# Two-layer sequence model on one core: input products one tile later, half of the condition blocks in the gate stage, the first chunk's outputs between the last two projections

## The chip, the cores and the metric

One Trainium2 chip, one of its cores. The metric is the device time of one execution in microseconds (us), the median of several runs. Engines: PE (TensorE, matrix products), DVE (VectorE), ACT (ScalarE), POOL (GpSimd), and SP, which only issues transfers. "PEld" is PE's weight load, a trailing q (SPq, ACTq) is the queue of an engine that issues DMAs.

## The reference

One sequence of 512 tokens of width 1024 in float32 goes through a gated delta-rule mixer, a SwiGLU feed-forward, an S5 mixer, a mixture of eight experts, and then two attention layers. The change touches the feed-forward, the S5 mixer and the gate behind it, and it computes the conditions of the two attention layers elsewhere:

```python
u = x @ w_in                                        # "projections"
a_bar = exp(lam * dt); bu = b_bar @ u               # per group: 16 channels, 64 complex states
h = associative scan of h[t] = a_bar * h[t-1] + bu[t]
y = real(c @ h) + d_skip * u
hid = gelu(y); val, gate = split(hid @ w_glu, 2)    # gate stage
x = layer_norm(ALPHA * x + val * sigmoid(gate))     # then router and experts
mods[layer] = silu(c) @ w_ada[layer] + b_ada[layer] # "condition", for attention layers 0 and 1
```

## The kernel before, in words

The kernel is a chain of stages. A stage (`Stage`) has one program for each engine; engines meet at its end. Semaphores (`then_inc`, `wait_ge`) order the engines inside it, and each engine works through its program strictly in the order in which it is written.

Matrix products of float32 precision are made in three passes (`three_pass`, L260 to L267): every weight tile is split into a high half (ACT, `split_hi`) and a low half (DVE, `split_lo`), and PE multiplies high by high, high by low and low by high. A weight tile that has no low half yet holds PE up.

**Feed-forward stage** (`dense_parts`, L2711). Two parts of 18 tiles each: 12 tiles "up" and 6 "down", numbered as splits 0 to 35. Beside the splits DVE does the work of `Parameters` (L1739), which prepares the S5 stage: after the low half of split n (`vector`, L1849) it does `condition` (blocks of the condition product: a 128x1024 piece of `w_ada` times `silu(c)` with a sum, L1975, two per split from split 9 on, 48 in all for both layers), and at the splits named in `Q_AT` and `P_AT` one of eight Q tables (`output_powers`, L1926) or P tables (`input_powers`, L1947). SP (`loads`, L2912) waits for each low half, then for the blocks and tables of that split, and issues their loads and stores and the next weight tile in that order. At the end `EndNorm` (L2632) normalizes the four token tiles one by one (`spread`, `centre` on DVE, `root` and `high_parts` on ACT, `turn` on PE, `low_parts` on DVE), and the last `turn` needs the last tile's norm.

**S5 stage** (`s5_layer`, L2025). Eight projections (`project`, L2092: one weight tile each, 24 matmuls), whose results ACT copies out (`copy_u`) and sends through DRAM to get them turned (`u_turn`, then `u_blk`, read back by SP's `turn_u`). Four chunks b follow, each with: `turn_tables` (16 transposes of its P table, inside a projection when `project` is given b), `inputs` (64 matmuls), `lags` (32), `outputs` (96) and `turn_back` (8 transposes). DVE scans the states (`turn_in`, `scan`, `turn_out`) and before that makes the rotation tables (`skip_diagonals`, `rotations`). POOL (`widen`, `zero`, `add_skip`) and SP (`place`) lay the lags out in `mix` by eight small DMAs each per chunk, which `outputs` reads. ACT fetches each chunk's P table (`next_tables`, once `inputs` of the chunk before are done) and Q block (`load_q`). PE's order is written out in L2157 to L2184.

**Gate stage** (`router`, L3405). Eight weight tiles (`s5_glu`), each multiplied with four token tiles; DVE does the low halves and the gated sums (`add`), then for the last chunk the norm (`spread`, `centre`), the router's logits and the slot lists. ACT does the sigmoids (`gate`). POOL has nothing to do in it.

`keep_busy` (L191) issues matmuls whose result nobody reads; each call is two records of a 128x384 product.

## Time and profile before

| | |
|---|---|
| median of 3 runs | 2575.66 us (2573.46 to 2578.72) |
| profiled execution, its own time | 2578.13 us |
| its span | 2576.4 us |
| PE busy | 2467.8 us, 96% of the span |
| DVE busy | 1740.6 us, 68% |
| ACT busy | 1044.0 us, 41% |
| POOL busy | 603.0 us, 23% |
| feed-forward stage | until about 844 us |
| S5 stage | 844 to 970 us |
| gate stage | 970 to 1082 us |

PE is busy nearly throughout, so the kernel's time is PE's work plus the holes in it, plus what PE takes longer where its granted clock is at the lower level. The views to read are therefore PE's waits by stage, and the timeline of the other engines just before each hole. Times in a timeline are counted from the start of the span; in brackets stands how long the engine was idle before and who released it.

### The profile page before, as it was taken

What the parts mean: (1) busy time and instruction counts of PE and PEld (TensorE: products, weight loads), DVE (VectorE), ACT (ScalarE), POOL (GpSimd) and SP (SyncE); (2) the same over time, 40 slices, a digit from 0 to 9 for tenths busy, and PEclk for the clock granted to TensorE, in tenths of its full rate; (3) what the DMA queues carried; (4) which work ended last, traced back from release to release, by engine and by line L of the source; (5) the groups of instructions that cost most, each with busy time, mean ns of one, the idle gap of its engine ahead of it and who ended that gap; (6) DMA issues with size and microseconds to landing.
All of it is one profiled execution on the core that took longest, in us unless ns stands there. A gap on an engine that the chain in (4) does not pass through costs nothing. (4 is left out here: it accounts for less than half of the span.)

```text
span 2576.4 us, 40971 instructions
## 1 busy us (share of the span) xinstructions
PE 2467.8 (96%) x15793; PEld 2031.6 (79%) x15793; DVE 1740.6 (68%) x2854; ACT 1044.0 (41%) x1561; POOL 603.0 (23%) x481
## 2 busy tenths in 40 slices
PE   8998989999999899899999999998999998999998
PEld 7788887787878689799999999886676576767576
DVE  7944656468888743666766766676687567487666
ACT  4443233331211342455555555443344452344453
POOL 2404321430230140142333432430024001024001
PEclk9999999999999899999999999999999999999999
DMA  4321002347664552367777777843221211332121
GB/s 156 91 89 36 2 3 66 118 137 259 207 212 162 183 157 85 105 224 238 239 250 228 235 244 228 287 167 125 86 74 60 76 68 56 110 94 70 33 82 66
DMA packets 265197, 348.33 MB, mean 135 GB/s; under 512 B 23184, under 2 KB 221008, under 8 KB 264528
## 3 DMA queue, kind: packets, MB, share of 16 engines
q1 hardware_dynamic: 253872, 313.81, 37.6%
q0 software_dynamic: 5536, 17.17, 2.0%
q10 hardware_dynamic: 5632, 15.21, 1.8%
q8 instruction: 104, 1.70, 0.3%
q14 instruction: 53, 0.43, 0.0%
HBM read 322.83 MB, written 20.71 MB: 133 GB/s over the span
## 5 line engine op out<-in xcount | busy, mean ns | idle before, releaser
L3057 PE MATMUL ps<-x_feat_r,moe_w_hi 128*128 128x384 f32 x1408 | 405.2, 361 | 2.6 <-DVE x_feat_r L3169 2.6
L2587 DVE TENSOR_TENSOR moe_w_lo<-ring,moe_w_hi 128x2048 fp32r<-128x2048 f32 x144 | 316.8, 2201 | 130.3 <-ACT moe_w_hi L2582 130.1
L3060 PE MATMUL ps<-x_feat_r,moe_w_lo 128*128 128x192 f32 x1408 | 354.0, 251 | 0.0
L2582 ACT ACTIVATE moe_w_hi<-ring 128x2048 fp32r<-128x2048 f32 x144 | 254.8, 1770 | 97.5 <-PE ps L263 60.8
L3060 PEld LDWEIGHTS ps<-x_feat_r,moe_w_lo 128*128 128x128 f32 x1408 | 269.2, 191 | 0.3
L3057 PEld LDWEIGHTS ps<-x_feat_r,moe_w_hi 128*128 128x128 f32 x1408 | 264.3, 188 | 3.7 <-issue 3.4
L267 PE MATMUL ps<-x_free_r,ring_r 128*128 128x512 f32 x496 | 195.6, 394 | 0.0
L266 PE MATMUL ps<-ring_r,x_feat_r 128*128 128x256 f32 (+2 forms) x576 | 183.9, 319 | 0.0
L263 PE MATMUL ps<-x_feat_r,ffn_w_hi 128*128 128x512 f32 x352 | 139.7, 397 | 1.2 <-DVE ffn_w_lo L2530 1.2
L267 PE MATMUL ps<-x_feat_r,ffn_w_lo 128*128 128x512 f32 x352 | 139.5, 396 | 0.0
L266 PE MATMUL ps<-x_free_r,ffn_w_hi 128*128 128x512 f32 x352 | 138.3, 393 | 0.0
L2582 ACT ACTIVATE ffn_w_hi<-ring 128x2048 fp32r<-128x2048 f32 (+1 forms) x35 | 61.8, 1769 | 176.3 <-PE ps L263 149.6
L4098 ACT ACTIVATE s_sb<-s_sb,att_small 128x512 f32<-128x512 f32 (+3 forms) x128 | 71.9, 562 | 133.2 <-DVE att_small L4090 133.0
L266 PEld LDWEIGHTS ps<-ring_r,x_feat_r 128*128 128x128 f32 x576 | 108.7, 189 | 7.8
L267 PEld LDWEIGHTS ps<-x_free_r,ring_r 128*128 128x128 f32 x496 | 93.1, 188 | 21.1
L3105 ACT ACTIVATE moe_cross<-ps 128x384 f32<-128x384 f32 (+1 forms) x96 | 44.4, 462 | 150.8 <-PE ps L3060 150.8
L263 PE MATMUL ps<-x_feat_r,acc_r 128*128 128x512 f32 x256 | 103.4, 404 | 0.0
L267 PE MATMUL ps<-x_feat_r,ring_r 128*128 128x512 f32 x256 | 101.7, 397 | 0.0
L266 PE MATMUL ps<-x_free_r,acc_r 128*128 128x512 f32 x256 | 101.6, 397 | 0.0
L3288 POOL TENSOR_TENSOR moe_hid_hi<-moe_prod,cst 128x384 fp32r<-128x384 f32 (+1 forms) x48 | 54.5, 1134 | 195.3 <-DVE moe_prod L3232 195.3
L4366 POOL TENSOR_TENSOR sq<-c_all 128x512 f32<-128x512 f32 x16 | 19.7, 1232 | 342.9 <-ACT c_all L3974 342.9
L194 PE MATMUL ps<-cst 128*128 128x384 f32 x226 | 83.7, 518 | 15.8 <-PEq L175 13.7
(654 smaller groups left out, 6401.9 us busy)
## 6 DMA issues: line engine op xcount, KB each, us to landing
ring<-in_moe_w SPq DMA_DIRECT2D x120, 1024.0 KB, 8.6
ring<-in_w_in SPq DMA_DIRECT2D x32, 1024.0 KB, 5.3
ring<-in_ffn_w SPq DMA_DIRECT2D x30, 1024.0 KB, 7.8
ring<-in_ada_t SPq DMA_DIRECT2D x48, 512.0 KB, 4.6
ring<-in_gdn_w_in SPq DMA_DIRECT2D x12, 1024.0 KB, 5.7
ring<-in_moe_w SPq DMA_DIRECT2D x24, 512.0 KB
ring<-in_s_w_glu SPq DMA_DIRECT2D x8, 1024.0 KB, 5.9
ring<-in_w_out SPq DMA_DIRECT2D x8, 1024.0 KB, 6.7
```

The lines of the kernel that those rows point to most:

```text
L194: prog.nc.tensor.matmul(prog.ps[:, bank, 0:3 * P], prog.ident, prog.cst, start=True, stop=True)
L263: m = nc.tensor.matmul(out, lh, rh, start=first, stop=False)
L266: nc.tensor.matmul(out, lh, rl, start=False, stop=False)
L267: return nc.tensor.matmul(out, ll, rh, start=False, stop=last)
L2582: self.prog.nc.scalar.activation(self.flat(self.hi, j % SPLITS, j), self.raw(j), ACT.Copy).then_inc(self.hi_done, 1)
L2587: self.prog.nc.vector.tensor_tensor(self.flat(self.lo, j % SPLITS, j), self.raw(j), self.flat(self.hi, j % SPLITS, j).bitcast(F32), ALU.su ...
L3057: mm = nc.tensor.matmul(out, wh[:, k, cs], both[:, k, :], start=(k == 0), stop=False)
L3060: mm = nc.tensor.matmul(out[:, 0:SLOTS], wl[:, k, cs], xg[0][:, k, :], start=False, stop=(k == KD - 1))
L3105: nc.scalar.activation(cross_of(c, which), half(c, which, 1), ACT.Copy).then_inc(cross_copied, 1)
L3288: nc.gpsimd.tensor_tensor(hi, src, prog.ones[:, 0:1].unsqueeze(2).to_broadcast([P, len(ms), SLOTS]), ALU.mult).then_inc(hi_ready, 1)
L4098: self.nc.scalar.activation(x, x, ACT.Exp, bias=self.small[:, u % 4, 1:2], scale=self.heads[h][3], accum_out=self.small[:, u % 4, 2:3]).th ...
L4366: m = nc.gpsimd.tensor_tensor(sq[:, 0 if first else 1, :], c_all[:, k, :], c_all[:, k, :], ALU.mult)
```

## The change

It does six things.

- `Parameters` computes only layer 0's 24 condition blocks, one per split (9 to 32), and the Q and P tables move to other splits; the first P table goes from split 11 to 13.
- `input_powers` walks its arrays with the channel innermost instead of the step.
- In `EndNorm`, ACT and DVE also split the S5 stage's first weight tile, and PE issues eleven `keep_busy` calls ahead of the last `turn`; the two at the head of the S5 stage go.
- In the S5 stage PE's order is: projections 0, 1, 2 (with chunk 0's tables), 3, `inputs(0)`, `lags(0)`, 4, 5 (tables 1), `inputs(1)`, `lags(1)`, 6, `outputs(0)`, 7 (tables 2), `inputs(2)`, `lags(2)`, tables 3 on their own, `turn_back(0)`, `inputs(3)` and the rest as before. ACT, DVE and SP follow.
- The gate stage gets layer 1's 24 condition blocks: POOL loads them, one DMA each into two buffers, DVE multiplies them in six groups of four, one group behind each low half from tile 2 to tile 7, and `finish_conditions` stands ahead of the norm.
- ACT applies silu to the condition row once more in the gate stage.

```diff
@@ Parameters
-    FIRST_SPLIT, PER_SPLIT = 9, 2
-    Q_AT = {9: 0, 13: 1, 17: 2, 20: 3, 23: 4, 26: 5, 29: 6, 32: 7}
-    P_AT = {11: 0, 15: 1, 19: 2, 22: 3, 25: 4, 28: 5, 31: 6, 34: 7}
+    FIRST_SPLIT = 9
+    Q_AT = {9: 0, 14: 1, 17: 2, 20: 3, 22: 4, 24: 5, 26: 6, 31: 7}
+    P_AT = {13: 0, 16: 1, 19: 2, 21: 3, 23: 4, 25: 5, 27: 6, 33: 7}
     def blocks_at(self, split):
-        first = (split - self.FIRST_SPLIT) * self.PER_SPLIT
-        return range(max(first, 0), min(max(first + self.PER_SPLIT, 0), DEPTH * self.BLOCKS))
+        n = split - self.FIRST_SPLIT
+        return range(n, n + 1) if 0 <= n < COND_BLOCKS else ()
@@ input_powers
-        shape = [P, self.QUADS, GC, STEP]
+        shape = [P, self.QUADS, STEP, GC]
...
-        p_re, p_im, tmp = self.p[:, 0], self.p[:, 1], self.p_tmp
+        p_re, p_im, tmp = (x.rearrange("p q c i -> p q i c") for x in (self.p[:, 0], self.p[:, 1], self.p_tmp))
@@ new, used by both stages (COND_BLOCKS is 24)
+def condition_block(prog, layer, n, weights, row):
+    return prog.nc.vector.scalar_tensor_tensor(out=weights, in0=weights, scalar=1.0, in1=row, op0=ALU.mult, op1=ALU.mult,
+                                               accum_out=prog.mods[:, layer, n:n + 1])
+def finish_conditions(prog, link, layer):
+    nc, mods, scale = prog.nc, prog.mods[:, layer, :], prog.mods[:, layer, KD:2 * KD]
+    link(nc.vector.tensor_tensor(mods, mods, prog.ada_par[:, layer, :], ALU.add))
+    link(nc.vector.tensor_scalar(scale, scale, 1.0, None, ALU.add))
@@ s5_layer, PE
-            keep_busy(prog, 7, 2)
             project(0)
             project(1)
             project(2, 0)
+            project(3)
             inputs(0)
-            project(3)
-            project(4, 1, lambda half: table_bank_free(0, half))
+            lags(0, lambda half: table_bank_free(0, half))
+            project(4)
+            project(5, 1, lag_bank_free)
             inputs(1)
-            lags(0, lambda half: table_bank_free(1, half))
-            project(5)
-            project(6, 2, lag_bank_free)
+            lags(1, lambda half: table_bank_free(1, half))
+            project(6)
+            outputs(0)
+            project(7, 2, lambda half: lag_bank_free(2 + half))
             inputs(2)
-            lags(1, lambda half: table_bank_free(2, half))
-            project(7, 3, lambda half: lag_bank_free(2 + half))
-            lags(2, lambda half: table_bank_free(3, half))
-            outputs(0)
-            turn_back(0, lambda half: lag_bank_free(4 + half))
+            lags(2, lambda half: table_bank_free(2, half))
+            turn_tables(3, 0, lambda half: lag_bank_free(4 + half))
+            turn_tables(3, 1, lambda half: pe.wait_ge(t_copied, 12 + half + 1))
+            turn_back(0, lambda half: table_bank_free(3, half))
             inputs(3)
@@ s5_layer, ACT (rewritten between copy_tables(0) and finish(0); only the new order)
+            copy_tables(0); copy_u(2); proj.split_hi(act, 5); copy_u(3); proj.split_hi(act, 6)
+            next_tables(1); load_q(1); copy_lags(0); copy_u(4); proj.split_hi(act, 7); copy_tables(1); copy_u(5)
+            next_tables(2); load_q(2); copy_lags(1); copy_u(6); copy_y(0); load_q(3); copy_tables(2); copy_u(7)
+            next_tables(3); copy_lags(2); copy_tables(3); finish(0)
@@ s5_layer, DVE
-            for n in range(3):
-                proj.split_lo(dve, n)
+            dve.sem_inc(proj.lo_done, 1)
+            proj.split_lo(dve, 1)
+            proj.split_lo(dve, 2)
             skip_diagonals()
             rotations()
             proj.split_lo(dve, 3)
             proj.split_lo(dve, 4)
+            proj.split_lo(dve, 5)
             turn_in(0)
-            proj.split_lo(dve, 5)
+            proj.split_lo(dve, 6)
             scan(0)
             turn_out(0)
-            proj.split_lo(dve, 6)
+            proj.split_lo(dve, 7)
@@ s5_layer, SP
             turn_u(5)
+            place(1)
             turn_u(6)
-            place(1)
             turn_u(7)
@@ EndNorm (ACT, DVE) and the end of the feed-forward stage (PE)
+    def split_next_hi(self, act):
...
+        self.nc.scalar.activation(self.next_hi, W.flat(NEXT, 0)[0], ACT.Copy).then_inc(self.next_hi_done, 1)
+    def split_next_lo(self, dve):
...
+        self.nc.vector.tensor_tensor(lo, x, self.next_hi.bitcast(F32), ALU.subtract)
...
+                pe.wait_ge(by_token.low_done, 2)
+                keep_busy(prog, 0, 11)
                 by_token.turn(pe, NT - 1)
@@ router, DVE
+                def conditions(first, count):
+                    for n in range(first, first + count):
+                        if n == 0:
+                            dve.wait_ge(silu_row, 1)
+                        dve.wait_ge(cond_landed[n % 2], 16 * (n // 2 + 1))
+                        condition_block(prog, DEPTH - 1, n, cond_w[:, n % 2, :], cond_row).then_inc(cond_used, 1)
+                each = COND_BLOCKS // (2 * LAST)
                 for c in range(LAST):
                     tiles.split_lo(dve, 2 * c + 2)
+                    conditions(2 * c * each, each)
...
                     tiles.split_lo(dve, 2 * c + 3)
+                    conditions((2 * c + 1) * each, each)
+                dve.wait_ge(cond_used, COND_BLOCKS)
+                finish_conditions(prog, link, DEPTH - 1)
@@ router, POOL
+                pool.dma_start(cond_row, inp["ada_c"]).then_inc(row_landed, 16)
+                for n in range(COND_BLOCKS):
+                    if n >= 2:
+                        pool.wait_ge(cond_used, n - 1)
+                    pool.dma_start(cond_w[:, n % 2, :], inp["ada_t"][DEPTH - 1, n * P:(n + 1) * P, :]
+                                   ).then_inc(cond_landed[n % 2], 16)
```

## Rows read from the trace of the kernel before

**Rows 1.** What TensorE (PE) waited for, 500 to 836 us: total us, times, longest

```profile
PE ps L263 <- DVE ffn_w_lo L2587: 4.4, 2, 2.9
```

**Rows 2.** Timeline of PE: start us, us, engine line op, out<-in, xcount, idle before

```profile
585.45 0.50 PE L263 MATMUL ps<-ffn_w_hi,ffn_hid_hi 128*128 128x512 f32 x1 [2.88 <-DVE ffn_w_lo L2587]
...
836.21 1.03 PE L2663 MATMUL ps<-cst,x_tok 128*128 128x128 f32 x8
...
846.75 1.11 PE L263 MATMUL ps<-x_feat_r,acc_r 128*128 128x512 f32 x1
...
963.66 6.62 PE L194 MATMUL ps<-cst 128*128 128x384 f32 x20
```

**Rows 3.** Windows of 2 us: PE, PEld, DVE, ACT, POOL busy (x), granted clock, DMA

```profile
586.00:588.00 2.00, 2.00 (x8) 1.57 (x7) 2.00 (x3) 1.91 (x1) 1.93 (x1) 0.72 0.00 0
588.00:590.00 2.00, 2.00 (x7) 1.51 (x6) 2.00 (x3) 0.00 (x0) 1.92 (x2) 0.50 0.82 231
590.00:592.00 2.00, 2.00 (x10) 1.64 (x9) 2.00 (x1) 0.00 (x0) 0.24 (x1) 0.93 0.63 147
```

**Rows 4.** What PE waited for, 836 to 975 us, columns as in Rows 1

```profile
PE ps L2109 <- DMA s_ublk<-u_turn: 6.5, 2, 3.4
PE ps L2663 <- DVE x_tok L2689: 3.7, 1, 3.7
...
PE ps L2154 <- ACT acc L2226: 1.4, 2, 0.7
PE ps L2122 <- POOLq L2404: 0.7, 1, 0.7
```

**Rows 5.** Timeline of ACT and PE in the S5 stage

```profile
854.07 1.11 ACT L2209 ACTIVATE s_uring<-ps 128x512 f32<-128x512 f32 x1 [5.03 <-PE ps L267]
...
859.62 1.13 ACT L2209 ACTIVATE s_uring<-ps 128x512 f32<-128x512 f32 x1 [2.88 <-PE ps L267]
...
870.29 3.56 PE L2109 MATMUL ps<-s_ublk,s_into 128*64 128x64 f32 x64 [3.45 <-DMA s_ublk<-u_turn]
...
910.07 2.09 PE L2109 MATMUL ps<-s_ublk,s_into 128*64 128x64 f32 x64
```

**Rows 6.** Timeline of DVE in the S5 stage

```profile
850.40 0.22 DVE L2314 TENSOR_TENSOR s_pow<-cst 128x64 f32<-128x64 f32 x1
...
868.40 2.36 DVE L3895 TENSOR_TENSOR ring_r<-ring,acc_r 128x1024 fp32r<-128x1024 f32 x2
```

**Rows 7.** Timeline of DVE in the feed-forward stage

```profile
573.16 2.06 DVE L1975 SCALAR_TENSOR_TENSOR ring<-ring,x_tok 128x1024 f32<-128x1024 f32 x1
...
577.40 1.13 DVE L1959 TENSOR_TENSOR x_tok<-s_bbar,s_pow 128x512 f32<-128x512 f32 x1
...
579.61 0.69 DVE L1961 TENSOR_TENSOR x_tok<-x_tok 128x512 f32<-128x512 f32 x1
...
814.42 0.69 DVE L2881 TENSOR_TENSOR acc<-ps,acc 128x512 f32<-128x512 f32 x1 [5.13 <-DMA s_p<-x_tok]
```

**Rows 8.** Timeline of DVE: a block in the feed-forward stage, then the gate stage

```profile
603.63 1.22 DVE L1975 SCALAR_TENSOR_TENSOR ring<-ring,x_tok 128x1024 f32<-128x1024 f32 x1
...
985.91 2.29 DVE L242 TENSOR_TENSOR ring_r<-ring,s_glu_hi 128x2048 fp32r<-128x2048 f32 x1 [9.04 <-ACT s_glu_hi L234]
989.85 0.42 DVE L3566 TENSOR_TENSOR s_sig<-s_sig,ps 128x256 f32<-128x256 f32 x1 [1.65 <-ACT s_sig L3680]
...
1043.16 2.29 DVE L242 TENSOR_TENSOR ring_r<-ring,s_glu_hi 128x2048 fp32r<-128x2048 f32 x1 [0.41 <-ACT s_glu_hi L234]
1049.70 0.42 DVE L3566 TENSOR_TENSOR s_sig<-s_sig,ps 128x256 f32<-128x256 f32 x1 [4.25 <-ACT s_sig L3680]
```

**Rows 9.** DMA issues of the whole execution: count, KB each, median us to landing

```profile
ring<-in_ada_t SPq DMA_DIRECT2D x48, 512.0 KB, 4.6
...
s_into<-s_p ACTq DMA_DIRECT2D x4, 1024.0 KB, 5.4
y_rows<-moe_y POOLq DMA_DIRECT2D x7, 512.0 KB, 3.5
```

More of the change, by code:

```diff
@@ L1951, in input_powers @@
         quad = slice(n * self.QUADS, (n + 1) * self.QUADS)
[L1952 to L1955 removed]
+        shape = [P, self.QUADS, STEP, GC]
+        b_re, b_im = (self.s5.bbar[:, r, quad, :].unsqueeze(2).to_broadcast(shape) for r in range(2))
+        re, im = (self.s5.pw[:, r, 1:].rearrange("p i q -> p q i")[:, quad, :].unsqueeze(3).to_broadcast(shape) for r in range(2))
+        p_re, p_im, tmp = (x.rearrange("p q c i -> p q i c") for x in (self.p[:, 0], self.p[:, 1], self.p_tmp))
         dve.wait_ge(self.q_done, n + 1)
@@ L1974, in condition @@
             dve.wait_ge(self.weights_landed[n % 2], 16 * (n // 2 + 1))
-            nc.vector.scalar_tensor_tensor(out=self.weights[n % 2], in0=self.weights[n % 2], scalar=1.0, in1=self.row,
-                                           op0=ALU.mult, op1=ALU.mult, accum_out=mods[:, layer, i:i + 1]
-                                           ).then_inc(self.weights_used, 1)
-            if n == DEPTH * self.BLOCKS - 1:
+            condition_block(self.prog, 0, n, self.weights[n % 2], self.row).then_inc(self.weights_used, 1)
+            if n == COND_BLOCKS - 1:
                 dve.wait_ge(self.weights_used, n + 1)
                 dve.wait_ge(self.bias_landed, 16)
-                link(nc.vector.tensor_tensor(mods, mods, self.prog.ada_par, ALU.add))
-                for l in range(DEPTH):
-                    scale = mods[:, l, KD:2 * KD]
-                    m = nc.vector.tensor_scalar(scale, scale, 1.0, None, ALU.add)
-                link(m)
+                finish_conditions(self.prog, self.linked(dve), 0)
+COND_BLOCKS = 3 * D // P
+def condition_block(prog, layer, n, weights, row):
[5 more added lines that the diff above has]
+    link(nc.vector.tensor_scalar(scale, scale, 1.0, None, ALU.add))
 def load_turned(sp, u_dram, u_blk, f, landed):
@@ L2629, in parts_of @@
             yield e
+NEXT = "s5_u"
 class EndNorm:
@@ L2644, in __init__ @@
         names = ("gamma_landed", "beta_landed", "norm_link", "var_ready", "sd_ready", "centred", "normed", "turned", "x_hi_done",
-                 "measured")
+                 "measured", "low_done", "next_hi_done")
         (self.gamma_landed, self.beta_landed, self.norm_link, self.var_ready, self.sd_ready, self.centred, self.normed,
-         self.turned, self.x_hi_done, self.measured) = (st.counter(n) for n in names)
+         self.turned, self.x_hi_done, self.measured, self.low_done, self.next_hi_done) = (st.counter(n) for n in names)
         self.link = None
+        self.next_hi = prog.split_scratch[:, 0, 0:D]
+    def split_next_hi(self, act):
+        W = self.prog.weights
+        act.wait_ge(self.normed, 1)
+        W.arrived(act, NEXT, 0)
+        self.nc.scalar.activation(self.next_hi, W.flat(NEXT, 0)[0], ACT.Copy).then_inc(self.next_hi_done, 1)
+    def split_next_lo(self, dve):
+        x, lo = self.prog.weights.flat(NEXT, 0)
+        dve.wait_ge(self.next_hi_done, 1)
+        self.nc.vector.tensor_tensor(lo, x, self.next_hi.bitcast(F32), ALU.subtract)
     def loads(self, sp):
@@ L2828, in scalar @@
                         end.high_parts(act, t - 1)
+                    if t == NT - 2:
+                        end.split_next_hi(act)
                 end.high_parts(act, NT - 1)
@@ L2886, in vector @@
                         end.low_parts(dve, t - 1)
+                    if t == NT - 2:
+                        end.split_next_lo(dve)
                 end.low_parts(dve, NT - 1)
@@ L3425, in router @@
         sig = prog.sbuf("s5_sig", [P, 2, UP_COLS], own)
+        cond_row = prog.sbuf("cond_row", [P, D], own)[:, :]
+        cond_w = prog.sbuf("cond_w", [P, 2, D], own)
         turned_logits = prog.sbuf("moe_turned", [EXPERTS, NT, P], own)
@@ L3459, in router @@
             pick, token, spot = gather
+            row_landed, silu_row, cond_used = st.counter("row_landed"), st.counter("silu_row"), st.counter("cond_used")
+            cond_landed = [st.counter(f"cond_landed_{i}") for i in range(2)]
             late = slice(0, SLOTS - P)
@@ L3695, in _ @@
                 tiles.split_hi(act, 1)
+                act.wait_ge(row_landed, 16)
+                nc.scalar.activation(cond_row, cond_row, ACT.Silu).then_inc(silu_row, 1)
                 for c in range(LAST):
```

43 lines of the change are left out of this document (17 added, 26 removed).

## The prediction

> **What bounds the kernel now.** I read three views, in this order: what TensorE (PE) waited for in each stage, then the timeline around each wait, then the windows with the granted clock. From 500 to 836 us, in the dense feed-forward stage, PE waits for one thing only: twice, 4.4 us together, for the low half of a weight tile that VectorE (DVE) makes late [rows 1]. The first of these stalls, 2.88 us, ends at 585.45, so the second is 1.5 us [rows 2]. Behind the first the granted clock is at the lower of its two levels, 1.2 GHz, for about 3.3 us (0.72, 0.50 and 0.93 in windows of 2 us) [rows 3]: some 1.7 us more. In the S5 stage the waits are 6.5 us in two for the turned input `u_blk`, 3.7 us for the norm of the last token tile, and small ones [rows 4]. So in both stages PE sets the end, and DVE or a transfer makes the holes. In the gate stage (`s5_glu`, 970 to 1082 us) PE is full until about 1067 us, DVE half idle at first, but from 1049.70 on DVE runs the norm, the router and the slot lists in one chain [rows 8]. A delay of DVE there is a delay of the kernel.
>
> **Feed-forward stage: fewer condition blocks, P tables elsewhere.** Before, the split that stalls PE was queued behind two blocks (2.06 and about 2.3 us) and a whole P table [rows 7]. Now one block stands there, and the first P table comes two splits later: the low half, which ended at 585.4, ends near 577.5, before PE's 582.6. The second stall is the same pattern (two blocks and Q number 6 ahead of it); the new lists leave splits 28 to 30 with one block each. What is late next at both places is the last product of the chunk, which the next matmuls need only 2.8 us (12 matmuls) on: no new wait. The Q and P tables now sit closer, in pairs from split 19 to 27. Per two tiles (22.2 us of PE) DVE has two splits, two blocks, a P and a Q and two products, some 20 us: it fits. The P table's new loop order writes with a stride where it read with one. No row has this pattern; a step lies between the 0.69 us of the contiguous one and the 1.13 us of the strided read [rows 7], so a table costs 4.2 to 6.8 us against 5.8. I take 5.8, and it is covered by DVE's slack of 2 us per pair at any value but the last. SP's stores follow the tables; the last one, for which DVE stood 5.13 us [rows 7], goes out some 15 us earlier, which PE does not feel. Sum: -2.9 - 1.5 - 1.7 = **-6.1 us** (bounds -6.6 and -4.4, the latter if the slow clock stays).
>
> **Into S5: eleven filler matmuls before the last turn.** Twenty records of the filler, ten calls, last 6.62 us [rows 2], so eleven last 7.3. They start behind turn(2), at 837.0, and end at 844.3, while the last tile's norm (delayed 0.4 us by the added 1.2 us split of the next tile, since DVE had 0.9 us of slack) is ready at 841.2. The last turn thus ends at 845.3 instead of 842.9, and the stage opens 2.7 us later, at 847.2. In exchange the first projection, which began at 846.75 on the lower clock [rows 2], finds its tile split already and runs at 2.4 GHz: 847.2 + 5.55 = 852.8 against 854.07 [rows 5], **-1.3 us** there.
>
> **S5: where the wait goes.** One projection is 5.55 us (854.07 to 859.62) and one with a chunk's tables inside 7.2 (859.62 to 866.84) [rows 5]. Projections 0, 1 and 2 end at 865.6. The new order puts projection 3 next, not the inputs, so the wait for `u_blk` is covered. But projection 3 needs the low half of tile 3, which DVE's program makes behind `skip_diagonals` and `rotations`: these took 18.0 us, from 850.4 to 868.4 [rows 6]. DVE now gets there at 851.8 (2.4 us later by the turn, 1.1 earlier because tile 0's pieces are gone), is through at 869.8, and tile 3 is ready at 871.0. PE waits **5.4 us**, in place of 3.45, and comes out on the lower clock: the 64 input matmuls behind the old hole took 3.56 us against 2.09 [rows 5], so 1.5 us again. Downstream: lags(1) needs GpSimd's (POOL's) second `widen`, which stands behind eight DMA issues: about 0.4 us. The tables of the fourth chunk no longer hide in projection 7. Their load is issued once inputs(2) are done, at 923.6, and takes 5.4 us [rows 9]; PE is through lags(2) at 927.2, so 1.9 us of waiting, and 0.8 us more because nothing fills the copies between their transposes. Sum of the new holes: 5.4 + 1.5 + 0.4 + 1.9 + 0.8 = 10.0. The old holes, all gone: 6.5 + twice 1.5 of clock + 0.7 (lags(2) on POOL) + 0.7 (the copy of y, which the outputs moved forward cover) = 10.9 [rows 4, 5]. With the -1.3 the stage gives **-2.2 us** (bounds -5, if the hole costs no clock and the load of tables lands in the 3.5 us that others take, and +1, if it stays slow for twice as long). On the queues: ACT now reads the tables of chunk 1 behind inputs(0), still 6 us ahead of their transposes, and the last Q blocks 18 us sooner; SP places chunk 1 ahead of `turn_u(6)`, which only inputs(3) need. Further on the lags of chunk 3 set the end by the same twelve us as before, and outputs(0) waits for nothing, because POOL and SP placed its lags 7 us earlier.
>
> **Gate stage: 24 blocks, loaded through POOL.** One block is 1.15 us of DVE, start to start, where POOL computes nothing [rows 8]; a group of four would be 4.6. But there are two buffers, and the load of block n+2 is issued only when block n has been read. The trace shows no load through POOL's queue; a store of the same 512 KB through it lands after 3.5 us, a block through SP's after 4.6 as median [rows 9]. I take 3.5, since it is the row of that queue and this stretch is quieter than that of the 4.6. The third block's load goes at 1.3 and lands at 4.8, the block ends at 5.95; the fourth, issued at 2.45, lands at 6.0 and ends at 7.2. So a group is **7.2 us**. From 988.2, where tile 2's low half ends, DVE has in a row: 6 groups 43.2, five splits of 2.29 = 11.5, twelve pairs of 0.42 + 0.43 = 10.1, the statistics 2.4, small ones 0.5, `finish_conditions` 0.6, together 68.3: it comes to the last chunk's sum at 1056.5, and with 0.4 to 0.7 us of further landing waits at 1057.2 instead of 1049.70 [rows 8]. On the way PE's last tile (its low half was ready at 1045.45) comes 3 us late, which costs nothing of its own, as DVE is later still. **+7.5 us.** Lower bound: loads land in time. Then DVE is bound by PE as before up to 1045.45, and only the last group and the finish, less the 4.25 us that DVE idled there, are added: +1.0. Upper: 4.6 us to landing, by the same walk +16. The Trainium skill, DMA: Bandwidth & Descriptors, section on the anatomy of a DMA on the gpsimd path, fits such a DMA as 2.0 us plus its bytes at 436 GB/s; for 512 KB that is 3.2 us (an estimate by that page), where the row says 3.5. By it the groups would cost 5.6 us in place of 7.5.
>
> **Sum.** -6.1 - 2.2 + 7.5 = -0.8 us. The profiled execution took 2578.13 us (span 2576.4), 2.5 above the median of 2575.66; it becomes 2577.3, and the median **2575 us**. What a measurement here tells from no change is about 0.2%, 5.2 us.
>
> **Rivals.** (1) The loads through POOL are never waited for: they land within 2.3 us, or as good as. Then -6.1 - 2.2 + 1.0 = -7.3: 2568.4. Against it, no 512 KB row lands so soon; for it, the stretch is quiet. 0.15. (2) No hole at projection 3, because DVE's rotations or the opening of the stage come sooner than I worked out, with the gate stage as in the forecast: 5.4 + 1.5 gone, -7.7: 2568.0. Against it the 18.0 us of [rows 6], a fixed run of DVE work. 0.15. (3) **Slower**: the second load of each pair shares the 16 engines with the first and with the gate weights and lands after 4.2 us or more. Groups become 7.9 to 8.3 us, tile 5 is late as well as tile 7, and the stage costs +13 to +16: total +5 to +8, 2581 to 2584. It decides from a landing of 4.2 us on; the 4.6 us median of SP's blocks speaks for it, the 3.5 of POOL's queue against. 0.24. (4) The change doesn't reach the path at all (the holes of DVE's lateness stay, the added work is hidden), a result near zero, goes with the forecast.
>
> **Chances.** Forecast and what lies within 5.2 us of no change 0.46; faster 0.30; slower 0.24. The range reaches to rival 1 with a little of the S5 bound, 2566.5, and into rival 3, 2583.
>
> **What would show it.** The two PE waits for `ffn_w_lo` gone; PE full until 844 us (less 6) with the clock at its higher level at the first projection; a PE wait of some 5 us for `ring_r` (L3895) before the fourth projection in place of those for `s_ublk`; a wait of 2 us for `s_into`; in the gate stage DVE waits for DMA, twice in each group, summing to some 15 us, and the router's chain 7 us later against its stage's start. It is wrong if DVE's rows show no wait for `cond_w`, or if PE enters the fourth projection without a hole.

## The result and the profile after

| | before | after |
|---|---|---|
| median, runs taken side by side | 2576.91 us | 2594.52 us |
| range of these runs | 2573.46 to 2578.72 | 2590.21 to 2597.23 |
| profiled execution, its span | 2576.4 us | 2590.8 us |
| first product of S5 | 846.75 | 841.38 |
| first product of the gate stage | 971.96 | 966.53 |
| last chunk's first gated sum | 1049.70 | 1064.40 |
| first product of the experts | 1096.34 | 1109.55 |

The changed kernel takes 1.0071 times as long, 95% interval 1.0058 to 1.0083: 17.6 us by the medians, 14.4 us between the two profiled executions. The forecast was 2575 us, no change. The four marks at the foot of the table, read from the two timelines, and the two spans say where it went: 5.4 us are gained by the time S5 starts and are kept through S5; the gate stage then loses 20.1 us (97.87 us from its first product to the last chunk's sum, against 77.74), of which 1.5 come back before the experts start; 1.2 are added in the rest.

In the feed-forward stage the two waits of [rows 1] are gone: the list of PE's waits from 500 to 830 us is empty. PE's waits from 836 to 975 us, after (total us, times, longest), against [rows 4]:

```profile
PE ps L263 <- DVE ring_r L3945: 5.5, 1, 5.5
PE ps L2092 <- DMA s_into<-s_p: 2.2, 1, 2.2
PE ps L263 <- DVEq L2372: 1.9, 1, 1.9
...
PE ps L2157 <- ACT acc L2230: 0.7, 1, 0.7
```

The waits for `s_ublk` are gone, and two new ones stand there, for the low half of tile 3 and for the fourth chunk's tables. The timeline of PE at the opening and at the first of these holes, with the windows around it (columns as in Rows 2 and 3), against [rows 2, 5]:

```profile
831.35 7.26 PE L194 MATMUL ps<-cst 128*128 128x384 f32 x22
838.45 1.04 PE L2684 MATMUL ps<-cst,x_tok 128*128 128x128 f32 x8
841.38 0.50 PE L263 MATMUL ps<-x_feat_r,acc_r 128*128 128x512 f32 x1 [1.90 <-DVEq L2372]
...
865.40 0.77 PE L263 MATMUL ps<-x_feat_r,acc_r 128*128 128x512 f32 x1 [5.47 <-DVE ring_r L3945]
...
873.67 2.09 PE L2112 MATMUL ps<-s_ublk,s_into 128*64 128x64 f32 x64
```

```profile
864.00:866.00 2.00, 0.60 (x2) 0.54 (x3) 1.97 (x2) 0.00 (x0) 0.00 (x0) 0.52 0.28 98
866.00:868.00 2.00, 2.00 (x6) 1.62 (x5) 1.92 (x4) 0.00 (x0) 0.00 (x0) 0.50 0.43 99
868.00:870.00 2.00, 2.00 (x6) 1.52 (x6) 0.00 (x0) 0.00 (x0) 0.00 (x0) 0.50 0.19 40
870.00:872.00 2.00, 2.00 (x9) 1.60 (x8) 0.00 (x0) 0.00 (x0) 0.00 (x0) 0.77 0.00 0
```

S5 now opens at the higher clock: its first matmul takes 0.50 us, where it was 1.11 in [rows 2]. Behind the hole the clock is at the lower level until about 871, so the fourth projection takes 873.67 - 865.40 = 8.27 us instead of 5.55.

The gate stage, DVE's waits from 975 to 1064 us, and the second group of four blocks on the timeline, with POOL's issues between DVE's rows, against [rows 8, 9]:

```profile
DVE cond_w L1981 <- DMA cond_w<-in_ada_t: 27.9, 15, 4.2
```

```profile
997.59 1.22 DVE L1981 SCALAR_TENSOR_TENSOR cond_w<-cond_w,cond_row 128x1024 f32<-128x1024 f32 x1
...
999.11 0.53 POOL L3717 DMA_DIRECT2D cond_w<-in_ada_t  x1 [6.80 <-DVE cond_w L1981]
...
1000.26 0.53 POOL L3717 DMA_DIRECT2D cond_w<-in_ada_t  x1 [0.62 <-DVE cond_w L1981]
1003.52 1.23 DVE L1981 SCALAR_TENSOR_TENSOR cond_w<-cond_w,cond_row 128x1024 f32<-128x1024 f32 x1 [3.56 <-DMA cond_w<-in_ada_t]
...
1005.56 1.23 DVE L1981 SCALAR_TENSOR_TENSOR cond_w<-cond_w,cond_row 128x1024 f32<-128x1024 f32 x1 [0.81 <-DMA cond_w<-in_ada_t]
```

The first two blocks are there. (That isn't so in the third and fifth group, which start right behind the one before.) The load of the third is issued at 999.11, 1.5 us into the group, and lands 4.4 us later; that of the fourth, at 1000.26, 5.3 later. The group ends at 1006.71, 9.1 us after its start. The six groups take 8.7, 9.1, 12.7, 8.6, 9.0 and 8.5 us. PE feels it twice, and behind both waits the granted clock is 0.50 (from 1028 to 1034 us and from 1054 to 1058):

```profile
1029.52 0.58 PE L263 MATMUL ps<-s_glu_hi,x_feat_r 128*128 128x256 f32 x1 [5.66 <-DVE ring_r L242]
...
1055.49 0.58 PE L263 MATMUL ps<-s_glu_hi,x_feat_r 128*128 128x256 f32 x1 [6.32 <-DVE ring_r L242]
```

And the transfers of the whole execution (count, KB each, median us to landing), against [rows 9]; the loads into `cond_w` land after 3.6 us at the least and 7.2 at the most:

```profile
cond_w<-in_ada_t POOLq DMA_DIRECT2D x24, 512.0 KB, 4.5
...
y_rows<-moe_y POOLq DMA_DIRECT2D x7, 512.0 KB, 3.5
```

### The profile page after: what moved, and what is told of

Same layout as the page of the kernel before. It is cut to its first block and busy times, and to the rows that moved or that the text cites. A ratio compares the mean times of both kernels' runs of the same rounds, so it can differ in the third digit from the quotient of the medians.

```text
span 2590.8 us, 41014 instructions
## 1 busy us (share of the span) xinstructions
PE 2477.2 (96%) x15811; PEld 2037.3 (79%) x15811; DVE 1752.9 (68%) x2852; ACT 1046.3 (40%) x1560; POOL 622.0 (24%) x506
## 5 line engine op out<-in xcount | busy, mean ns | idle before, releaser
L194 PE MATMUL ps<-cst 128*128 128x384 f32 x244 | 89.8, 516 | 13.7 <-PEq L175 11.6
```

What stands on the lines that cost most here:

```text
L194: prog.nc.tensor.matmul(prog.ps[:, bank, 0:3 * P], prog.ident, prog.cst, start=True, stop=True)
```

## The experiments

The landing of a transfer is here the time from its issue until its data are there. The theory was that the 20 us of the gate stage are landings, and nothing else: a block's load can be issued only when the block two before it has been read, and four blocks stand in a row. Its rivals were the 24 multiplications themselves (24 times 1.15 us of DVE) and contention of the loads with the gate weights. For S5 the theory was that DVE's order (tile 3 behind the rotations) makes the hole, and the clock a second cost. Each ratio is to the kernel before on the same chip, with its 95% interval; a difference in us is the ratio's distance from 1 times 2577. Beside it stands a length from the traces: S5, from its first product to the gate stage's first (125.21 us before, 125.15 after), or the gate stage, from its first product to the last chunk's first sum (77.74 and 97.87). The gate stage of one program repeats within 0.1 us from trace to trace where no block waits. S5 doesn't: the changed kernel and experiments 1 to 4 have the same S5 program, and there it is 125.15, 125.19, 125.50, 124.35 and 123.55 us long, since the lower clock behind its waits lasts longer in some of them.

**1. Nothing of the blocks in the gate stage.**

```diff
-                    conditions(2 * c * each, each)
...
-                    conditions((2 * c + 1) * each, each)
-                dve.wait_ge(cond_used, COND_BLOCKS)
+                link(nc.vector.memset(prog.mods[:, DEPTH - 1, :], 0.0))
```

> The changed kernel without anything of the 24 condition blocks in the gate stage: no loads through POOL, no multiplications, no silu of the row; layer 1's conditions are set to zero plus their bias, so they are left out of the computation. The rest of the change stays. Theory (landings cost it): all of the 20.1 us that the gate stage grew by goes, 2594.5 - 20 = 2574.5 us, 2.4 less than the kernel before, since of what the feed-forward and the opening gained (5.4) part is lost elsewhere. Rival (the forecast's sum holds for the rest: -6.1 and -2.2): 2576.9 - 8.3 = 2568.6. Rival (the lateness comes from somewhere else in the change, such as the S5 order): above 2585.

Measured: 0.9984 (0.9975 to 0.9992), -4.1 us. The gate stage is 77.77 us long, as before. All of its growth is the blocks', and the rest of the change gains 4.1 us (2.1 to 6.4), not the 8.3 of the forecast.

**2. The multiplications without the loads.** One block is loaded and read 24 times, written to two scratch slots in turn.

```diff
-                        dve.wait_ge(cond_landed[n % 2], 16 * (n // 2 + 1))
-                        condition_block(prog, DEPTH - 1, n, cond_w[:, n % 2, :], cond_row).then_inc(cond_used, 1)
+                        dve.wait_ge(cond_landed[0], 16)
+                        nc.vector.scalar_tensor_tensor(out=cond_w[:, 1 + n % 2, :], in0=cond_w[:, 0, :], scalar=1.0, in1=cond_row,
...
```

> As the changed kernel, but only one of the 24 blocks is loaded in the gate stage; DVE makes all 24 multiplications from it, so the work of DVE is whole and no block waits for a landing (layer 1's conditions are those of one block, so 23 of 24 are left out of the computation). Theory (landings): a group of four takes 4.6 to 5.3 us instead of 8.5 to 12.7, and the stage costs 1 to 2 us over the run without blocks: 2576. Rival (the 24 multiplications themselves, 28 us of DVE work, are the cost): 2588 or more.

Measured: 0.9981 (0.9972 to 0.9989), -4.9 us; the gate stage is 78.52 us long. A group is 4 times 1.15 = 4.6 us, as the timeline of DVE in this run shows:

```profile
983.83 1.22 DVE L3639 SCALAR_TENSOR_TENSOR cond_w<-cond_w,cond_row 128x1024 f32<-128x1024 f32 x1
...
987.27 1.22 DVE L3639 SCALAR_TENSOR_TENSOR cond_w<-cond_w,cond_row 128x1024 f32<-128x1024 f32 x1
988.41 0.09 DVE L3639 DVE_READ_ACCUMULATOR cond_w<-cond_w,cond_row 128x1 f32 x1
988.41 0.42 DVE L3597 TENSOR_TENSOR s_sig<-s_sig,ps 128x256 f32<-128x256 f32 x1
```

So 27.6 us of DVE work cost 0.75 us of the stage: they fall into DVE's idle time there. The rival of the work is out.

**3. Four buffers.** Everything is loaded and computed; only the ring is longer.

```diff
+COND_RING = 4
...
-        cond_w = prog.sbuf("cond_w", [P, 2, D], own)
+        cond_w = prog.sbuf("cond_w", [P, COND_RING, D], own)
...
-                    if n >= 2:
-                        pool.wait_ge(cond_used, n - 1)
+                    if n >= COND_RING:
+                        pool.wait_ge(cond_used, n - COND_RING + 1)
```

> The changed kernel with four buffers for the blocks in the gate stage instead of two; everything is loaded and computed. Theory (landings that two buffers leave no time for): the four loads of a group are issued while DVE does the splits and the additions of the stretch before, so no or nearly no wait for a landing is left: 2576 to 2578. Rival (the loads contend with the gate weights and are late however early they are issued, or delay the weights): DVE's waits for the blocks stay over 10 us or PE waits for s_w_glu; 2585 or more.

Measured: 0.9977 (0.9967 to 0.9987), -5.9 us. The stage is 78.53 us long. DVE's waits from 975 to 1050 us hold none for a block:

```profile
DVE ring_r L242 <- ACT s_glu_hi L234: 16.0, 4, 9.0
DVE s_sig L3598 <- ACT s_sig L3729: 3.4, 3, 1.1
```

though the loads land later than with two buffers (5.2 us as median, 10.8 the longest, with up to four in flight). A landing costs only where it can't be issued early. The rival of contention is out as the cause of the 20 us; it is real as a part of the size, below. No run loaded the blocks through another queue, so what POOL's queue itself adds isn't shown.

**4. Three buffers**, the same edit with 3.

> The changed kernel with three buffers for the blocks of the gate stage; all is loaded and computed. Theory (a landing is paid each time that a block's load can be issued only inside its own group): now one block in four waits, for a load issued 1.2 us into the group that lands after 4.5 to 5 us, so a group takes some 6.9 us where four buffers gave 4.6 and two 8.5 to 12.7. By the same walk through the stage as in the forecast, the last chunk's sum comes 84 to 86 us behind the stage's first product (78.5 with four buffers, 97.9 with two), and the whole lies 5.4 to 7.5 us above the run with four buffers: within 0 to 2 us of the kernel before. Rival (two loads in flight on POOL's queue slow each other, and three do so more): no better than 90 us in the stage, 6 us slower than before or more.

Measured: 0.9996 (0.9987 to 1.0006), -1.0 us; the stage is 82.52 us long, 4.0 more than with four. DVE waits for blocks again, from 975 to 1060 us:

```profile
DVE cond_w L1982 <- DMA cond_w<-in_ada_t: 12.0, 8, 2.3
```

The size was a little over-estimated (84 to 86 us), the order of the three is as the theory has it: 97.9, 82.5, 78.5 us with two, three and four.

**5. Tile 3 first.**

```diff
+            proj.split_lo(dve, 3)
             skip_diagonals()
             rotations()
-            proj.split_lo(dve, 3)
```

> The changed kernel with the low half of tile 3 of the S5 projection made by DVE ahead of skip_diagonals and rotations instead of behind them. Theory (the 5.47 us of PE before the fourth projection, and the 2.7 us that it then loses at the lower clock, come from that place alone): 2594.5 - 8 = 2586.5, if nothing else is late next. Rival (what follows is set by DVE's and POOL's chain of the chunks, which starts only when the rotations are made, 1.2 us later here): the hole moves to the inputs or the lags and the time stays within 3 us of 2594.5.

Measured: 1.0029 (1.0018 to 1.0040), +7.5 us against the kernel before, 10.8 less than the changed kernel's 18.3. S5 is 118.14 us long, 7.0 less. PE's waits from 836 to 975 us no longer have the hole, and the one for the tables has grown from 2.2 to 3.2:

```profile
PE ps L2092 <- DMA s_into<-s_p: 3.2, 1, 3.2
PE ps L263 <- DVEq L2372: 1.9, 1, 1.9
```

The hole (5.5) and the clock behind it (2.7) less the 1.0 of the other wait are these 7. The rival, that the chain of the chunks holds the time, is out. That the ratios differ by 10.8 us and the stage by 7.0 isn't explained.

**6. Both repairs**, four buffers and tile 3 first.

> Both repairs: four buffers for the blocks of the gate stage, and tile 3's low half ahead of skip_diagonals and rotations. All is computed. Theory (the two are in series on one path): -5.9 from the first and -10 from the second by their runs against the kernel before and after, 7.0 of the latter seen in the S5 stage of its trace: 13 to 16 us faster than the kernel before. Rival (the second was worth something only because the gate stage was late anyway): 8 to 10 us faster.

Measured: 0.9959 (0.9946 to 0.9972), -10.6 us; S5 116.16 us, the gate stage 78.50. The ratio lies between the two expectations. By the stage lengths the two repairs add: S5 is 8.2 us shorter than with four buffers alone, and the gate stage stays at 78.5. By the ratios they don't quite: 5.9 of the four buffers leave 4.7 for the order, where experiment 5 had 10.8. The intervals are 2.6 to 3.4 us wide to either side, and no run settles it.

**7. The hole filled, not removed**, on the kernel with four buffers.

```diff
             project(2, 0)
+            keep_busy(prog, E_BANK, 8)
             project(3)
```

> The changed kernel with four buffers, and eight filler matmul calls (20 records were 6.62 us, so eight calls are 5.3) in TensorE's hole of 5.5 us before the fourth projection. The wait for tile 3 stays. Theory (the 2.7 us that the fourth projection lost are the lower clock behind the idle time, a second cost beside the wait): the granted clock stays at its higher level from 860 to 872 us, the projection takes 5.55 us in place of 8.27, and the kernel is 2 to 3 us faster than the one with four buffers alone (-5.9 against the kernel before): -8 to -9. Rival (the projection was slow because its operands were late, not for the clock; or the 2.7 us come back in the waits for DVE and the tables further on): -6.

Measured: 0.9991 (0.9982 to 1.0000), -2.3 us: nothing gained on the four buffers' -5.9, and rather some lost. The clock did what was expected at the hole. PE's timeline and the windows of this run:

```profile
859.48 5.32 PE L194 MATMUL ps<-cst 128*128 128x384 f32 x16
865.14 0.47 PE L263 MATMUL ps<-x_feat_r,acc_r 128*128 128x512 f32 x1 [0.34 <-DVE ring_r L3947]
...
870.87 2.09 PE L2113 MATMUL ps<-s_ublk,s_into 128*64 128x64 f32 x64
...
923.50 3.77 PE L2093 MATMUL ps<-cst,s_into 128*128 128x128 f32 x16 [3.95 <-DMA s_into<-s_p]
```

```profile
866.00:868.00 2.00, 2.00 (x11) 1.61 (x9) 1.67 (x4) 0.00 (x0) 0.00 (x0) 1.00 0.40 91
...
924.00:926.00 2.00, 2.00 (x11) 1.77 (x9) 1.97 (x3) 1.10 (x2) 1.96 (x5) 0.50 0.76 157
```

The clock stays at its higher level over the hole, and the fourth projection takes 870.87 - 865.14 = 5.73 us. So what it lost in the changed kernel was the clock. How much that is differs from trace to trace: 2.7 us in the changed kernel and in experiments 1 and 2, but 1.7 in the runs with four and with three buffers, here the one with four:

```profile
865.64 0.76 PE L263 MATMUL ps<-x_feat_r,acc_r 128*128 128x512 f32 x1 [5.50 <-DVE ring_r L3946]
...
872.90 2.08 PE L2113 MATMUL ps<-s_ublk,s_into 128*64 128x64 f32 x64
```

So the filler gained 1.5 us against that run, and not 2.7. But S5 is 124.93 us long, against 124.35. What was gained came back 50 us later: PE waits 3.95 us for the fourth chunk's tables instead of 2.3, because their load landed 7.5 us after its issue (5.8 with four buffers, and as much in the changed kernel), and it was followed by the lower clock. It is the slowest landing of this load in all the traces (5.3 to 6.7 in the others); whether by chance or because more transfers ran beside it can't be told from one execution. The 3.6 us that the ratio lies above that of experiment 3 aren't in the edited stages: from S5's first product to the last chunk's sum the two traces differ by 0.6 us.

**8. The feed-forward part alone**, added to the kernel before: the new `Parameters` and nothing else (the P table's loop order is not shown here; layer 1's conditions are left out).

```diff
-    FIRST_SPLIT, PER_SPLIT = 9, 2
+    FIRST_SPLIT = 9
...
-    Q_AT = {9: 0, 13: 1, 17: 2, 20: 3, 23: 4, 26: 5, 29: 6, 32: 7}
-    P_AT = {11: 0, 15: 1, 19: 2, 22: 3, 25: 4, 28: 5, 31: 6, 34: 7}
+    Q_AT = {9: 0, 14: 1, 17: 2, 20: 3, 22: 4, 24: 5, 26: 6, 31: 7}
+    P_AT = {13: 0, 16: 1, 19: 2, 21: 3, 23: 4, 25: 5, 27: 6, 33: 7}
```

> The kernel before with the change's feed-forward part alone: one condition block per split, the new places of the Q and P tables, the P table's new loop order. The opening of S5, its order and the gate stage are those of before; layer 1's conditions are left out (set to zero plus their bias). Theory: the forecast's feed-forward term, -6.1 us against the kernel before (2.9 and 1.5 of stalls and 1.7 of clock), with no wait of TensorE for ffn_w_lo from 500 to 830 us. Rival (the stalls come back at other splits, with the tables in closer pairs and dearer): -3 or less. The run without gate blocks, 4.1 us faster than before, then leaves +2 for the new opening and order of S5, where the forecast had -2.2.

Measured: 0.9974 (0.9965 to 0.9983), -6.7 us, with 6.1 forecast. The run without gate blocks has -4.1, so opening and order of S5 together cost 2.6 us by the ratios; the intervals are 2 us wide to either side. The traces put it at 0.3: from the feed-forward's second to last turn to the gate stage's first product it is 135.75 us before and 136.05 after. The other traces with the same program spread around that: 136.20 here, with the old opening and order, and 136.09, 136.40, 135.25 and 134.45 in experiments 1 to 4, with the new. A gain of 2.2 is in none of them.

**9. Six filler calls instead of eleven**, on both repairs.

```diff
-                keep_busy(prog, 0, 11)
+                keep_busy(prog, 0, 6)
```

> Both repairs (four buffers, tile 3 first) and the filler ahead of the feed-forward's last turn cut from eleven calls to six. Theory (the filler is longer than the wait it covers: in the trace with both repairs it runs from 829.26 to 836.5 us, while the last tile is normed at 833.2): the last turn starts 3.1 us sooner, S5 opens at about 836.2 instead of 839.29 after its start, still at the higher clock, and the kernel gains 3 us on the run with both repairs, which was 10.6 us faster than the kernel before: -13 to -14. Rival (the clock falls once the filler ends, or the next waits take the 3 us back): -9 to -11, with a granted clock under 1 between 833 and 845 us.

Measured: 0.9942 (0.9928 to 0.9955), -14.9 us. PE's timeline of this run:

```profile
830.02 1.03 PE L2685 MATMUL ps<-cst,x_tok 128*128 128x128 f32 x8
830.89 4.04 PE L194 MATMUL ps<-cst 128*128 128x384 f32 x12
834.88 1.09 PE L2685 MATMUL ps<-cst,x_tok 128*128 128x128 f32 x8
837.87 0.50 PE L263 MATMUL ps<-x_feat_r,acc_r 128*128 128x512 f32 x1 [1.90 <-DVEq L2373]
```

From the turn at 830.02 to S5's first product it is 7.85 us; with eleven calls it was 10.90 (828.39 to 839.29 in the run with both repairs). That is 3.05 us of filler with nothing to cover, and the first matmul is at the higher clock here too (0.50 us).

**10. outputs(1) ahead of the fourth chunk's tables**, on both repairs.

```diff
             lags(2, lambda half: table_bank_free(2, half))
+            outputs(1)
             turn_tables(3, 0, lambda half: lag_bank_free(4 + half))
...
             inputs(3)
-            outputs(1)
             lags(3, lambda half: turn_bank_free(0, half))
```

> Both repairs, and outputs(1) ahead of the fourth chunk's tables instead of behind inputs(3). Theory (the forecast's hole for the tables' load is real and can be covered): outputs(1) take 5.6 us, the load lands 5.8 to 7.5 us after its issue, so the gap of 2.4 us ahead of the tables and the smaller one of 0.3 are gone, and with them the lower clock behind them (1 us): 3 to 4 us faster than with both repairs alone, -14 against the kernel before. Rival (the end of S5 is set by the chain inputs(3), scan(3), outputs(3), which now starts later by outputs(1) less the gap, 3 us): the hole moves to outputs(3) and the time is that of both repairs or up to 2 us more.

Measured: 0.9942 (0.9928 to 0.9956), -14.9 us. The wait of 2.4 us for the tables' load is gone, and S5 is 114.95 us long instead of 116.16: 1.2 us of the 3 to 4 expected. PE's waits from 836 to 975 us show a new one, for the bank that lags(3) write and ACT's gelu frees:

```profile
PE ps L2126 <- ACT s_hid L2244: 1.0, 1, 1.0
...
PE ps L2093 <- ACT s_into L2197: 0.3, 1, 0.3
```

2.4 us are removed and 1.0 is new; the two of 0.3 behind ACT's copies stay. The 1 us of clock was not to be had: behind the wait of 2.4 us in the run with both repairs the granted clock is 1.00. That rested on other runs, where the clock did fall at this place.

**11. All four repairs.**

> All four: four buffers, tile 3 first, six filler calls, outputs(1) ahead of the tables. Theory: the two new ones add, 6 to 7 us faster than with both repairs, -16 to -18 against the kernel before (0.993 to 0.9938 of it). Rival: as for the two alone, one of them gives nothing, -13 to -14.

Measured: 0.9940 (0.9927 to 0.9954), -15.5 us: 2563.02 us against 2580.13 of the kernel before beside it. All is computed. It is the fastest of the kernels here, if not measurably so against the last two: the trace has the opening of experiment 9 (7.85 us) and the S5 of experiment 10 (115.06 us). The sum expected, 16 to 18, was too high by what experiment 10 lacked.

**12. The P table in the old loop order**, on both repairs.

```diff
-        shape = [P, self.QUADS, STEP, GC]
+        shape = [P, self.QUADS, GC, STEP]
...
-        p_re, p_im, tmp = (x.rearrange("p q c i -> p q i c") for x in (self.p[:, 0], self.p[:, 1], self.p_tmp))
+        p_re, p_im, tmp = self.p[:, 0], self.p[:, 1], self.p_tmp
```

> Both repairs, and the P table with the loop order of the kernel before (an operation then reads with a stride and writes in one piece). Theory (the table costs DVE 7.0 us with the new order, 5.8 with the old, and DVE's slack in the feed-forward covers either): no difference to the run with both repairs, -10 to -12 against the kernel before, and six operations of 5.8 us in sum in the trace. Rival (the tables in closer pairs leave no slack, or the dearer ones delay SP's stores): 1 to 4 us faster, since the stage's end comes sooner.

Measured: 0.9953 (0.9939 to 0.9966), -12.1 us, the same as both repairs without it within the interval. S5 is 117.97 us long here, 1.8 more than in experiment 6. That isn't the table: the clock fell at the opening, in spite of the eleven filler calls, and 1.6 of the 1.8 us are lost there (windows as in Rows 3):

```profile
842.00:844.00 2.00, 2.00 (x6) 1.51 (x6) 1.98 (x2) 0.94 (x1) 0.00 (x0) 0.50 1.02 412
```

DVE's groups of the table's first and last operation in this run (500 to 840 us; busy us, mean ns):

```profile
L1956 DVE TENSOR_TENSOR x_tok<-s_bbar,s_pow 128x512 f32<-128x512 f32 x8 | 13.2, 1648 | 0.0
...
L1961 DVE TENSOR_TENSOR x_tok<-x_tok 128x512 f32<-128x512 f32 x8 | 5.5, 692 | 0.3
```

The six means sum to 6.3 us a table. In the changed kernel the last of them is 1.26 us and the six sum to 8.0 (from start to end 6.9 to 7.1 us for four of the tables, 8.2 to 9.0 for the other four, whose first operations take over 2 us). That is 1.7 us of DVE per table for nothing, hidden in full.

A limit of all this: behind the last chunk's first sum all kernels run the same instructions, yet the fourteen profiled executions took between 1526.4 us (the changed kernel) and 1535.6 us (experiment 7) from there to their end. A single trace can't show a gain of a few us in the total. The gate stage's own length can: it is 78.50 to 78.53 us in the eight runs that have the multiplications and in which no block waited. S5's length can show one only beyond its own spread of 2 us, or where the waits inside it are read one by one.

## Why the prediction was wrong, point by point

**Feed-forward, -6.1: right, but for the price of the P table.** Both waits and the lower clock behind the first are gone; the last but one turn comes at 830.48 instead of 836.21, -5.7 in the trace, and the part alone gives -6.7 by its ratio. The P table was taken at 5.8 us with bounds of 4.2 and 6.8; it costs 8.0 as a mean and 6.9 at the least, outside them. The step that failed in it is "a step lies between the 0.69 us of the contiguous one and the 1.13 us of the strided read": the new order makes even the operations that read and wrote in one piece walk with a stride, 1.26 us instead of 0.69. It cost nothing, as the forecast said of any value but the last.

**Opening, -1.3: right.** The filler ends at 838.6 (844.3 less 6.1 was forecast), the stage opens at the higher clock, and ACT's copy of the first product starts at 847.16 instead of 854.07: -6.9, of which 5.7 are the feed-forward's, so -1.2 is the opening's. (Experiment 8 has the old opening, and from the last but one turn to this copy it takes 17.83 us, as before with 17.86; the new opening takes 16.68.) The 2.7 us of later opening that the forecast set against the clock are there and need not be: experiment 9 takes five calls away and 3.05 us with them.

**S5, -0.9 beside the opening: no gain came.** From the copy of the first product to the gate stage's first product it is 119.37 us instead of 117.89, +1.5; in the four other traces with this S5 program (experiments 1 to 4) the difference to before is +1.5, +1.8, +0.7 and -0.1. The holes are where they were put, and of the size: 5.47 us before the fourth projection (5.4 forecast), 2.2 and 0.2 at the tables (1.9 and 0.8), none at lags(1) (0.4). What was mis-sized is the clock. The term "so 1.5 us again" was read off 64 short matmuls behind a hole of 3.5 us; behind 5.5 us of idleness, with a whole projection following, the lower clock lasts to 871 and takes 2.7 (1.7 in two other traces). And the wait for the tables has its own lower clock, which the sum didn't have (changed kernel, windows as in Rows 3):

```profile
926.00:928.00 2.00, 2.00 (x9) 1.70 (x10) 1.93 (x3) 1.03 (x3) 2.00 (x5) 0.50 0.85 191
```

From the first of these transposes to `inputs(3)` it is 4.77 us here and 3.77 in the run with both repairs, where the clock didn't fall. That is 1.0 us more; as the waits for the copies in between are 0.3 shorter, 1.3 are the clock's. With these the new holes come to 5.5 + 2.7 + 2.5 + 1.3 = 12.0 instead of 10.0. Against the old ones, 10.9, that makes 1.1 of the +1.5; the last 0.4 aren't accounted for.

**Gate stage, +7.5: this is what made the forecast wrong; 20.1 measured.** The mechanism is the forecast's, two buffers and a load that can only be issued inside its own group, and the experiments bear it out from both sides: without loads +0.8, with four buffers +0.8, with three +4.8, with two +20.1. The lower bound of +1.0 was right; the term between the bounds was not. The step that failed is the landing of a block: "I take 3.5, since it is the row of that queue". That row is a store from a queue with one transfer in flight. And "the trace shows no load through POOL's queue" is not so. The list of transfers of the kernel before has 16 gathers of 128 or 64 rows of 1024 floats (512 or 256 KB), which POOL issues in pairs; they landed after 4.3 us at the soonest (here the median, as in Rows 9; the view gives no KB for a gather):

```profile
moe_rows_in<-x_rows,moe_spot POOLq DMA_INDIRECT x16, 4.8
```

Their 4.8 us and the 4.6 of SP's blocks both spoke for the dearer value. The blocks' loads landed after 3.6 us at best, 4.5 as median and 7.2 at worst. Of two loads issued 1.2 us apart the second takes longer: in the four groups that start with both blocks in place, the third block is used 3.8 to 4.4 us after its issue and the fourth 4.7 to 5.3. In the second group the third block's load takes 4.4 us from its issue and the fourth's, issued 1.2 us behind it, 5.3. Third: 1.5 + 4.4 = 5.9; fourth: 2.7 + 5.3 = 8.0, plus 1.15 is the group's 9.1 us, where the forecast had 7.2. The six groups sum to 56.6 us against 43.2 in the forecast, and these 13.4 count nearly in full (12.6), since DVE has no idle time left and PE waits for it. The range's upper end for this stage, +16, was too low as well, since it held one landing of 4.6 for all. The third group took 12.7 us. Its fourth block waited for this load, here on POOL's and DVE's timeline and in the windows of 4 us (DMA's share is the last but one column):

```profile
1013.26 0.53 POOL L3717 DMA_DIRECT2D cond_w<-in_ada_t  x1 [1.47 <-DVE cond_w L1981]
...
1020.50 1.23 DVE L1981 SCALAR_TENSOR_TENSOR cond_w<-cond_w,cond_row 128x1024 f32<-128x1024 f32 x1 [4.21 <-DMA cond_w<-in_ada_t]
```

```profile
1014.00:1018.00 4.00, 4.00 (x36) 4.00 (x35) 1.23 (x2) 0.00 (x0) 0.53 (x1) 1.00 1.00 347
```

7.2 us from issue to landing, with the 16 engines full: SP had issued a gate weight tile of 1 MB at 1012.54, 0.7 us before. The Trainium skill, DMA: Bandwidth & Descriptors, section "Issuing engines are not separate DMA queues", says that transfers of all issuing engines run on the same 16 DMA engines and interleave; the trace agrees, with these 7.2 us. The forecast weighed the fit for one DMA that the Trainium skill has on the same page, in its section on the anatomy of a DMA on the gpsimd path; it gives 3.2 us for this size (an estimate by that page). The trace doesn't bear it out for these loads: the least of the 24 is 3.6.

**The rivals.** Rival 3 named the cause, the place and the point from which it decides (4.2 us), and the median landing passed that point. It gave +13 to +16 for the stage, where 20.1 came, because it too let all loads land alike. Rivals 1 and 2 are out by the rows. The weighing between the 3.5 of another transfer on the same queue and the 4.6 of the same transfer on another queue went by the queue; the size, the direction and the company of the transfer were the better guide. (In the changed kernel SP's 24 blocks of the feed-forward land after 3.9 us as median, where they took 4.6 before: one kind of transfer on one queue has no fixed landing.)

**The sum.** -5.7, -1.2, +1.5, +20.1, then -1.5 up to the experts' first product and +1.2 behind it, are the 14.4 us between the two traces. The medians are 17.6 apart; the 3 us between lie within what executions of one kernel differ by behind the gate stage, and no run here settles them.

## What to carry to other kernels

Work moved into an engine's idle time is as cheap as its loads are early: 27.6 us of VectorE work cost 0.8 us with four buffers and 20 with two, so count for each load the time from the moment its buffer comes free to its use, and set it against the landing of the same kind of transfer in the same company, the slowest rather than the median. A hole of TensorE has two prices, the wait and, in most of these traces, the lower clock behind it. Filling it with idle matmuls gave back the second where it was filled, but the stage was no shorter in that trace, since a load further on landed late; one trace doesn't show whether that would be so again. And before an engine's long chain goes ahead of a short operation, ask who waits for the short one: 1.2 us put ahead of 18 took 7 us off the stage.

## What the runs showed of the hardware that was not expected

- After a short wait the lower clock comes or does not, and the length of the wait alone doesn't tell which. At the fourth chunk's tables it came behind 2.2 us (changed kernel), 2.5, 2.3, 2.3, 3.2 and 3.9 (experiments 1, 2, 3, 5 and 7). It stayed at 1.00 behind 2.8, 2.4, 1.9 and 2.7 (experiments 4, 6, 9 and 12). Where it came, it took 0.8 to 1.7 us more up to the next inputs.
- Filler matmuls over the hole of 5.5 us kept the clock at 1.00 there. At the opening of S5 eleven calls kept it up in nine of ten traces and six calls in both of theirs; experiment 12 is the one in which it fell.
- An elementwise DVE operation on 128x512 float32 takes 0.69 us with all its operands in one piece, 1.10 with one read over a stride, and 1.25 with reads and write over a stride. The Trainium skill, SBUF — State Buffer, section Specifications (TRN2), the row on cachelines, says that an access which leaves a line of 16 bytes each time pays a penalty; the rows agree, and put it at 0.4 to 0.6 us for this shape. The 0.69 and the 1.25 are the same subtraction; the 1.10 is a product whose other operand repeats one value.
- A 512 KB load through POOL's queue landed after 3.6 us at the soonest, alike with two, three and four buffers; the median went from 4.5 with two in flight (4.2 in experiment 5) to 4.8 with three and 5.2 with four.
